# A two-layer hybrid decoder step on one core: three operations of sampled attention at other places, and part of the merge of prompt attention on GpSimd

## The reference, cut to what matters

```python
def _compress(rows, w1, b1, w2):            # keys (0) and values (1) of the cache, in blocks
    ...
        h = h + jnp.einsum('bnsgd,sde->bnge', seg[:, i:i + n_cmp], w1[...])
    return jnp.einsum('bnge,ef->bngf', jax.nn.silu(h), w2)     # second layer

o_cmp, imp = _nsa_compressed(q, pos, k_c, v_c)                 # value product of the compressed branch
idx = _nsa_select(imp, pos, ...)                               # which 16 blocks of 64 rows
o_sel = _nsa_sel_attend(q_rot, pos, kg, vg, kpos)
o_win = _window_attend(q_rot, pos, keys, values, kpos_w)
no = gate[:, :, 0] * o_cmp + gate[:, :, 1] * o_sel + gate[:, :, 2] * o_win
no = no.reshape(B, T, NSA_WIDTH) * jax.nn.silu(pr['nsa_g'])
```

## Time and profile before

| | us |
|---|---|
| three runs of the kernel | 2413.56, 2417.15, 2418.44 (median 2417.15) |
| the profiled execution, its own time | 2425.19 |
| its span, first to last instruction | 2423.7 |
| TensorE busy | 2078.8 (86%) |
| TensorE weight loads | 1421.0 (59%) |
| VectorE busy | 1086.4 (45%) |
| ScalarE busy | 850.0 (35%) |
| GpSimd busy | 419.1 (17%) |
| mean granted TensorE clock | 0.896 of full |

### The profile page before, as it was taken

One profiled execution on the slowest core, in us unless ns is written; L12 is line 12 of the kernel. 1 busy time (PEld: TensorE's weight loads), 2 busy tenths in 40 slices (PEclk: granted clock), 3 DMA queues, 4 the chain that ended last, 5 costly groups with the idle time before them and its releaser, 6 DMA issues. The chain is left out here.

```text
span 2423.7 us, 35163 instructions
## 1 busy us (share of the span) xinstructions
PE 2078.8 (86%) x11656; PEld 1421.0 (59%) x11656; DVE 1086.4 (45%) x2800; ACT 850.0 (35%) x1918; POOL 419.1 (17%) x648
## 2 busy tenths in 40 slices
PE   6989967888888999986879998688888799999977
PEld 3645456767766666664345444577777566666543
DVE  2254275666544443443222543646565444444432
ACT  2211203334345555551222112134343455555512
POOL 0120001101133334420001100010011433443100
PEclk9999967979978999997979998689698899999878
DMA  5452010000067767753045521000000876787331
GB/s 179 156 183 80 26 48 15 1 10 1 1 161 186 181 162 180 193 125 118 1 150 167 182 70 41 17 14 1 10 1 2 195 180 166 179 193 183 91 118 39
DMA packets 173052, 242.57 MB, mean 100 GB/s; under 512 B 50714, under 2 KB 132282, under 8 KB 172192
## 3 DMA queue, kind: packets, MB, share of 16 engines
q1 hardware_dynamic: 143328, 146.81, 22.8%
q0 software_dynamic: 29536, 93.43, 14.0%
HBM read 223.23 MB, written 25.50 MB: 103 GB/s over the span
## 5 line engine op out<-in xcount | busy, mean ns | idle before, releaser
L609 PE MATMUL bank<-W,hT 128*128 128x512 f32 (+3 forms) x1152 | 453.6, 546 | 17.6 <-DMA W<-in_w_in 12.7
L609 PEld LDWEIGHTS bank<-W,hT 128*128 128x128 f32 x1152 | 219.9, 197 | 209.4 <-issue 173.9
L978 PE MATMUL bank<-XT,W 128*128 128x256 f32 (+1 forms) x768 | 255.1, 463 | 0.0
L1218 POOL TENSOR_TENSOR work<-UP,SHARED 128x512 f32<-128x512 f32 x56 | 72.2, 1294 | 832.7 <-DVE UP L1503 504.0
L1233 ACT ACTIVATE Pr<-bank,mx 128x31 f32<-128x31 f32 (+4 forms) x192 | 85.6, 446 | 339.5 <-DVE mx L1428 330.2
L1035 POOL DMA_DIRECT2D SHARED<-in_cache_nsa_kv x256 | 152.8, 598 | 288.3 <-DVE RP L948 101.5
L1035 POOL DMA_DIRECT2D PS<-in_cache_nsa_kv x256 | 150.6, 588 | 269.3 <-issue 228.1
L978 PEld LDWEIGHTS bank<-XT,W 128*128 128x128 f32 x768 | 133.3, 190 | 56.2 <-issue 41.6
L960 PE MATMUL bank<-CF,RP 128*128 128x128 f32 x1024 | 153.1, 299 | 15.1 <-DVE RP L948 14.1
L967 ACT ACTIVATE XT<-bank 128x512 f32<-128x512 f32 x256 | 140.5, 596 | 47.2 <-PE bank L960 46.7
L960 PEld LDWEIGHTS bank<-CF,RP 128*128 128x128 f32 x1024 | 129.7, 155 | 21.8 <-DVE RP L948 18.1
(11 more groups left out here) (434 smaller groups left out, 3625.4 us busy)
## 6 DMA issues: line engine op xcount, KB each, us to landing
SHARED<-in_cache_nsa_kv SPq DMA_DIRECT2D x256, 128.0 KB, 4.4
SHARED<-in_cache_nsa_kv POOLq DMA_DIRECT2D x256, 128.0 KB, 4.4
PS<-in_cache_nsa_kv SPq DMA_DIRECT2D x256, 128.0 KB, 5.1
PS<-in_cache_nsa_kv POOLq DMA_DIRECT2D x256, 128.0 KB, 4.7
W<-in_w_in SPq DMA_DIRECT2D x48, 512.0 KB, 3.7
XS<-scratch_conv_p POOLq DMA_DIRECT2D x24, 384.0 KB, 4.6
PW<-in_state_nsa_win SPq DMA_DIRECT2D x16, 512.0 KB, 3.8
Wo<-in_w_out SPq DMA_DIRECT2D x4, 2048.0 KB, 11.9
```

Of the source, the lines that this page charges most:

```text
L609: return nc.tensor.matmul(bk((c * NTILE + t) % BANKS)[:, 0:b - a], hT[:, k, t * P:(t + 1) * P], W[:, k // 2, k % 2, 0:b - a], start=(k == ...
L978: mm = nc_(self.v).tensor.matmul(out, self.v['W1'][:, kv, s, :], seg[:, s], start=(s == 0), stop=(s == SEG // PAIRS - 1))
```

## The change

In `sample_attention` TensorE's list gets five other places; nothing is added or left out: C1 moves from j = 0 to j = 1, behind sc, the turn of maxima, kt2 and `T(4)`; `cpv` from j = 1 to j = 2; `combine` of the last sequence from j = 3 to j = 4; `cnb` now stands ahead of values of '3' with all of `halves` before it, `csb` behind. C1's bank of PSUM becomes that of scores '0'. VectorE's list is reordered to suit: `keep` of C1 behind the selection (`bi`), `nb` before `R8`, `co` behind `R9`, the window's maxima and `R10 R11` before `weighted`. ScalarE's list is not touched. In `delta_attention` VectorE keeps the three small instructions of a merge, which no longer wait for `merged` but for exponentials long done; GpSimd does the rest in four instructions, and its masks are put into one list with the merges.

```diff
@@ delta_attention
-    fac = sb(scope, "fac", [P, 2, 3])
+    fac = sb(scope, "fac", [P, 2, 2, 3])
+    mask_after = {}
+    for t, k in steps:
+        i = steps.index((t, k))
+        at = [ORDER.index(("ready2", t))] + ([ORDER.index(("turn", steps[i - 1]))] if i else [])
+        mask_after[ORDER[max(at)]] = (t, k)
@@ gpsimd
-            for i, (t, k) in enumerate(steps):
+            def mask(t, k):
...
+            def merge(k):
+                qt, br, h = units[GROUP * (k + 1) - 1]
+                first = h - 1
+                e.wait_ge(merged, k + 1)
+                e.wait_ge(scaled, k + 1)
+                link(nc.gpsimd.tensor_tensor(OB[:, :, :, :], OB[:, :, :, :], b_(fac[:, k % 2, :, :], 3, [P, 2, 3, HD]), ALU.mult))
+                link(nc.gpsimd.tensor_tensor(NO[:, :, :], OB[:, :, 0, :], OB[:, :, 1, :], ALU.add))
+                nc.gpsimd.tensor_tensor(NO[:, :, :], NO[:, :, :], OB[:, :, 2, :], ALU.add).then_inc(freed, 1)
+                e.wait_ge(freed, k + 1)
+                link(nc.gpsimd.tensor_tensor(MIX[:, qt, 256 + first * HD:256 + (first + 2) * HD], NO[:, :, :].rearrange("p h d -> p (h d)"),
+                                             U[qt][:, NG + first * HD:NG + (first + 2) * HD], ALU.mult))
+            for what, x in ORDER:
+                if (what, x) in mask_after:
+                    mask(*mask_after[what, x])
+                if what == "unit" and x >= BACK and (x - BACK) % GROUP == GROUP - 1:
+                    merge((x - BACK) // GROUP)
             dve.wait(e, "n33")
             first_pages(e, A, l, v, 1)
@@ vector, unit
-                    e.wait_ge(merged, k + 1)
-                    link(nc.vector.tensor_scalar(fac[:, :, :], SUM[:, k % 2, :, :], 1e-30, None, ALU.max))
...
-                    link(nc.vector.tensor_tensor(OB[:, :, :, :], OB[:, :, :, :], b_(fac[:, :, :], 3, [P, 2, 3, HD]), ALU.mult))
-                    nc.vector.tensor_reduce(NO[:, :, :], OB[:, :, :, :].rearrange("p h b d -> p h d b"), AX.X, ALU.add).then_inc(freed, 1)
...
+                    e.wait_ge(exped, GROUP * (k + 1))
+                    if k >= 2:
+                        e.wait_ge(freed, k - 1)
+                    link(nc.vector.tensor_scalar(fac[:, k % 2, :, :], SUM[:, k % 2, :, :], 1e-30, None, ALU.max))
+                    link(nc.vector.reciprocal(fac[:, k % 2, :, :], fac[:, k % 2, :, :]))
+                    nc.vector.tensor_tensor(fac[:, k % 2, :, :], fac[:, k % 2, :, :], gates, ALU.mult).then_inc(scaled, 1)
@@ sample_attention, tensor
+        for cp in cps:
+            cp.SECOND = (6, SCORES['0'])
-                    if a and j == 0:
-                        cb_.second(e, pe, act, dve, 1)
                     if j < 7:
                         T(2 * j + 2)
...
                     if a and j == 1:
+                        cb_.second(e, pe, act, dve, 1)
+                        window_turn(b)
+                    if p > 0 and j == 1:
+                        max_back(b - 1)
+                    if a and j == 2:
                         dve.wait(e, f"C1.{b}")
                         dve.wait(e, f"sf.{b}")
...
                         pe.done(e, f"cpv.{b}", mm)
-                    if p > 0 and j == 3:
+                    if p > 0 and j == 4:
                         combine(b - 1)
...
+                if c:
+                    cq.halves(e, pe, act, 1, (6, 8))
+                    dve.wait(e, f"cnd.{q}")
+                    pe.done(e, f"cnb.{q}", ...)
                 if a:
                     values(b, '3')
                 if c:
-                    cq.halves(e, pe, act, 1, (6, 7))
-                    dve.wait(e, f"cnd.{q}")
-                    pe.done(e, f"cnb.{q}", ...)
-                    cq.halves(e, pe, act, 1, (7, 8))
```

More of the change, by code:

```diff
@@ L1181, in delta_attention @@
         ends[what, t] = dn[-1]
[L1183 to L1184 removed]
+    mask_after = {}
[3 more added lines that the diff above has]
+        mask_after[ORDER[max(at)]] = (t, k)
+    with stage(["dve_s", "act_s", "pe_s", "loaded", "gl", "outs", "kv", "score", "shift", "exped", "turned", "copied", "used", "link_s", "merged", "freed", "masked", "scaled", "pool_s"]) as \
+            (block, (dve_s, act_s, pe_s, loaded, gl, outs, kv, score, shift, exped, turned, copied, used, link_s, merged, freed, masked, scaled, pool_s)):
         dve, act, pe = Steps(dve_s, dn), Steps(act_s, an), Steps(pe_s, pn)
@@ L1211, in _, with link @@
         def _(e):
-            for i, (t, k) in enumerate(steps):
-                n = ROWS[t]
+            links = [0]
+            def link(ins):
+                links[0] += 1
+                ins.then_inc(pool_s, 1)
+                e.wait_ge(pool_s, links[0])
+            def mask(t, k):
+                n, i = ROWS[t], steps.index((t, k))
                 dve.wait(e, f"nt1{t}")
@@ L1629, in sample_attention @@
         for j in range(8):
-            names_pe += at(f"kt{j+1}" if j < 7 else "") + (at("C1") if j == 0 else []) + co(f"T{2*j+2} T{2*j+3}" if j < 7 else "")
-            names_pe += {0: at("sc") + pr("mt"), 1: at("cpv wt") + pr("mb"), 2: at("Sw"), 3: at("S0") + pr("cb"), 4: at("tw S1"), 5: at("vw t0"),
+            names_pe += at(f"kt{j+1}" if j < 7 else "") + co(f"T{2*j+2} T{2*j+3}" if j < 7 else "")
+            names_pe += {0: at("sc") + pr("mt"), 1: at("C1 wt") + pr("mb"), 2: at("cpv Sw"), 3: at("S0"), 4: pr("cb") + at("tw S1"), 5: at("vw t0"),
                          6: at("S2 v0"), 7: at("t1")}[j]
-        names_pe += at("S3 v1 t2") + (["t0"] if not c else []) + co("H0") + at("v2") + co("C0 c4") + at("t3") + co("cmt") + at("v3") + \
-            co("cnb H1 csb")
+        names_pe += at("S3 v1 t2") + (["t0"] if not c else []) + co("H0") + at("v2") + co("C0 c4") + at("t3") + co("cmt H1 cnb") + at("v3") + \
+            co("csb")
         names_act += at("kt0 HS1") + co("X0 X1")
@@ L1639, in sample_attention @@
         names_act += at("c2 x3") + co("HT0 HS0") + at("c3") + co("ce HT1")
-        names_dve += pr("ms") + co("R4 R5") + pr("mb") + at("vn C1 sf t1 r1 t2 r2 bi") + co("R6 R7") + at("co0 co1") + pr("nb") + co("R8 R9") + \
-            pr("wl ls ow os") + co("R10 R11") + at("mn mw nw") + pr("ot0 ot1 lt") + at("m0 n0") + co("R12 R13") + at("m1 n1") + co("R14 R15") + \
+        names_dve += pr("ms") + co("R4 R5") + pr("mb") + at("vn sf t1 r1 t2 r2 bi C1") + co("R6 R7") + pr("nb") + co("R8 R9") + at("co0 co1") + \
+            at("mn mw nw") + co("R10 R11") + pr("wl ls ow os") + at("m0 n0") + pr("ot0 ot1 lt") + co("R12 R13") + at("m1 n1") + co("R14 R15") + \
             at("ew m2 n2 e0 m3 n3 e1") + co("A0") + at("e2") + co("C0") + (nx("R0 R1 R2 R3") if a else []) + co("cx0 cm cnd cnm cs0 cps") + at("e3") + \
@@ L1859, in _ @@
                         pe.done(e, f"cpv.{b}", mm)
[L1860 to L1863, removed]
                         window_scores(b)
@@ L1918, in _ @@
                     pe.done(e, f"cmt.{q}", nc.tensor.transpose(bk(C_AT)[0:COLS, 0:P], MX[:, :], ident))
+                if c:
+                    cq.halves(e, pe, act, 1, (6, 8))
+                    dve.wait(e, f"cnd.{q}")
+                    pe.done(e, f"cnb.{q}", nc.tensor.matmul(bk(C_AT)[:, P:P + COLS], v['ones'][0:COLS, :], nd[:, :], start=True, stop=True))
                 if a:
```

22 lines of the change are left out of this document (8 added, 14 removed).

## The result

| | before | after |
|---|---|---|
| median of the runs beside each other (range) | 2417.8 us (2413.6 to 2422.1) | 2352.1 us (2348.1 to 2356.4) |
| profiled execution (its span) | 2425.2 us (2423.7) | 2351.8 us (2350.5) |
| mean granted clock of TensorE | 0.896 | 0.912 |

The ratio is 0.973, with an interval of 0.970 to 0.975; on another chip the same pair gave 0.973 (0.969 to 0.977).

What follows compares the result with a forecast made beforehand. TensorE was taken as the bound, through its idle time and half clock. Sampled attention −18, merges −19, stage end +16 and clock −4 gave −25 us, from 2417 to 2392 us, range 2372 to 2418.

Steps and rivals of the forecast that it cites:

- The clock: TensorE's half clock: fewer stalls should mean fewer such stretches, −4 us, between −20 and +8.
- Rival C: Half clock stays away behind one prompt-stage stall and behind the fold: 16 to 20 us more, 2375; chance 0.17.
- The merge's idle time: Prompt's stage: moving merge work to GpSimd shortens stalls behind merges, −19 us over two layers, between −6 and −26.
- Sampled attention: Sampled attention, both layers: moving C1 and the fold gives −18 us, between −28 and −5.
- the fold: Sampled attention: one position later, its wait is nearly covered, −1.5 us a pass, between 0 and −1.65.
- C1: Sampled attention: one position later, T(2) waits behind the same silu instead, costing +0.3 us a pass.
- the end's order: Sampled attention's pass end: new places of cnb and csb change 0, from −0.3 to +0.3 us a pass.
- The tail: Prompt's stage end: GpSimd's page fetches now stand behind its last merge, +8 us a layer, +16 in all.
- The sign that was named: Prompt's stage end: the next stage's first instruction comes 10 us behind the last OB copy instead of 4.
- A: Slower: GpSimd's list ends the prompt's stage, inner gain stays under 4 us a layer; 2426 us, chance 0.10.
- B: No change: sampled attention's stalls only move, −18 becomes −3 and the clock 0; 2412 to 2417 us, chance 0.13.
- D: Sampled attention: all 14 waits before C1 vanish because X0 comes earlier, −19 us more; 2374 us, chance 0.05.

Runs made afterwards that it cites:

- e7: Changed kernel, with VectorE also doing three operations of the merge's sizes on its own buffers, without waiting for OB; 0.978 of the kernel before.
- e12: Changed kernel with cnb and the last two groups of H1 behind the last value product again, as before the change; 0.973 of the kernel before.
- e3: Changed kernel with GpSimd's wait for n33 and eight page fetches ahead of its last two merges; 0.967 of the kernel before.
- e2: Kernel before with only the prompt's merge moved to GpSimd, sampled attention unchanged; 0.988 of the kernel before.
- e5: Kernel before with only the fold moved to its later place; 0.988 of the kernel before.
- e4: Kernel before with only C1 and cpv moved to their later places; 0.996 of the kernel before.

## Why the prediction was wrong, step by step

- **The clock: -4 forecast, about -54 measured** (-52 by the time at half clock). This is the step that failed: "Fewer stalls should mean fewer such stretches ... I take −4, between −20 and +8." and the earlier trace rows carried the mechanism. What was missing was the amount at stake: at a granted clock of 0.87 the prompt's stage spends 2 x 0.13 x 322 = 84 us of a layer at half clock, and half of them, 42, are lost. Over both layers the time at half clock fell by 104 us, where the prediction called itself wrong from 20 on. Rival C, at 0.17, named the right mechanism. Its stretch begins behind a stall of 2.3 us that ends 5 us after a merge; in all ten layers with the merge on VectorE 10 to 17 us at half clock followed it at once, and the changed kernel has neither. The stall, then TensorE over the same work before and after:

```profile
515.54 0.30 PE L1295 MATMUL bank<-CF,Pr 128*128 128x128 f32 x1 [2.33 <-ACT PT L1247]
```
```profile
515.50:533.20 17.70, 16.46 (x65) 13.07 (x65) 9.09 (x25) 4.62 (x20) 2.44 (x2) 0.52 0.00 0
```
```profile
511.70:524.90 13.20, 10.86 (x67) 8.88 (x66) 7.43 (x23) 4.42 (x20) 4.30 (x6) 0.87 0.01 2
```

That this stall alone draws the stretch isn't shown: e7's first layer has it back with 2.01 us, and only 3.4 us at half clock follow, 3 us later. And C counted this stretch and the dips behind the fold, 16 to 20 us in all; its 2375 is still 23 us too long.
- **The merge's idle time, -19 forecast: -16 measured** (2 x 8.0). Going through the stalls gave the right size. Matmul by matmul, eleven waits of a layer lost 12.1 us; the one at 551.35, 1.69 us, is gone and the last, 2.08, is down to 0.98. What the forecast left out is that waits come up elsewhere: two of 1.0 us each, at 80 and 113 us into the stage, and others, 5.0 in all. GpSimd's merge took 2.4 us where 2.9 were worked out from the earlier trace rows: 384 columns took 0.83, 128 took 0.45.
- **Sampled attention, -18 forecast: -18 of idle time** (2 x 9.1), and another -22 of busy time, some 17 of them by the clock. That the first two agree is in part luck: a clean pass lost 1.8 us where 1.2 were forecast. By step: the fold -1.45 a pass (forecast -1.5); C1 +0.04 (+0.3); the end's order -0.36 (0, between -0.3 and +0.3); the first pass -4 (0), mostly half clock behind the wait for pages, though e12, with both moves, kept 53.1 of 54.6, so its cause stays open; behind the last csb -2.4 (-2).
- **The tail, +16 forecast: +20.** The mechanism held (e3 takes 8.7 of the 9.9 a layer away). The sum ended at GpSimd's last fetch plus the old hop. From the fetches' end (675.9) to the next stage's first matmul (680.6) are 4.7 us, where VectorE's last instruction and that matmul were 2 us apart before; why the hop is longer behind the fetches no run shows. The sign that was named, a first instruction 10 us behind the last `OB` copy, doesn't fit the forecast's own sum, which gives 12; it came 14.2 us behind that copy's end.
- **Rivals.** A (the tail eats the gain, GpSimd holds VectorE up) falls with e2: the gain inside the stage is 21 us a layer there (319.3 to 297.9), where less than 4 would have decided for A. B (the stalls only move) holds for C1, whose wait T(2) took over at 1.95 as forecast, and falls for the fold, whose wait of 1.65 is down to 0.24 in e5 and moved nowhere. D is refuted by e4: the waits ahead of C1 went to T(2), all of them.

## What to carry to other kernels

Before costing a removed stall, take TensorE's time at half clock in its stage, 2 x (1 - granted clock) x length: half of that is the most that stalls can cost beyond their own idle time. In the prompt's stage it was 45 us beside 46 of idle time, and of this change's gain the larger part came from it. Not all of it can be had: the 17 to 23 us at half clock of the stage's opening stayed in every run. Work that moves to an idle engine is cheap in the middle and dear at the end; look at what its list held last (here the next stage's fetches), and put that first. Where a stage's length has two values in profiles of the same code, compare like with like, and take a second profile before explaining a difference.

## What the runs showed of the hardware

- Half clock does not follow one stall in proportion. The same 1.3 us wait was followed by 3 us at half clock, or by a second wait and then 14; which of the two came went with a shift of 1.9 us some 50 us earlier.
- Giving back a wait, or 1.5 us of VectorE's work for each merge, cost the prompt's stage about 5 us a layer, of which 0.5 were idle time on average (2.5 at most, in one layer).
- Forty-three useless transposes in the right gaps made a stage of 298 us 10 us shorter; 121 made it 5.5 shorter. In the time of the kernel each was worth some 6 us of 2300, within the intervals.
- The same projection took 271 and 282 us in the two profiles of the kernel before: 257 and 264 us of TensorE's work at granted clocks of 1.00 and 0.97, and 13 and 18 us of idle time. What settles that is open.
